# Two-layer transformer on one core: the sparse attention step reorganised around stacked query rows

## What is computed

```
proj = x @ w_q                                   # 1024 -> 1024 query columns + 48 gate columns
q = rmsnorm_2(proj[..., :1024].reshape(..., G, HG, dh), q_norm)        # 4 groups x 4 heads of 64
gates = sigmoid(proj[..., 1024:])                                      # per head and branch
s_c = q @ k_c.T * scale + head_bias(rel_c);  p_c = softmax(mask(s_c));  o_c = p_c @ v_c
s_s = q @ k_sel.T * scale + bias_s;          p_s = softmax(mask(s_s));  o_s = p_s @ v_sel
s_w = q @ k_wb.T * scale + head_bias(rel_w); p_w = softmax(mask(s_w));  o_w = p_w @ v_wb
out = (gates[0] * o_c + gates[1] * o_s + gates[2] * o_w) @ w_o;   h = h + out
```

## Time and profile before

| | us |
|---|---|
| median of 3 runs | 2265.68 |
| lowest and highest | 2264.12, 2272.57 |
| the profiled execution, own time | 2275.57 |
| its span, first to last instruction | 2274.3 |
| PE busy | 2192.8 (96%) |
| DVE busy | 1207.8 (53%) |
| ACT busy | 1012.2 (45%) |
| POOL busy | 15.5 (1%) |
| mean granted clock of TensorE | 0.96 of 2.4 GHz |

### The profile page before, as it was taken

The page is one execution under the profiler, slowest core; times in us unless marked ns, Lnnn a source line. Parts: engine busy times, 40 slices in busy tenths (PEclk is TensorE's granted clock), DMA queues, the critical chain, the costliest instruction groups (busy, mean ns, idle before and its releaser), DMA issues.

```text
span 2274.3 us, 25942 instructions
## 1 busy us (share of the span) xinstructions
PE 2192.8 (96%) x10555; PEld 1801.3 (79%) x10555; DVE 1207.8 (53%) x1350; ACT 1012.2 (45%) x1320; POOL 15.5 (1%) x33
## 2 busy tenths in 40 slices
PE   8998999999999999999999999999999998999999
PEld 6887987888888766888888798788768876768887
DVE  5455686545554645644654565545545554345544
ACT  6444345445444555534544433444444443435443
POOL 1000000000000000000000000000000000000000
PEclk9999999999999999999999999999999996558999
DMA  7553436564664522655565446756366541104653
GB/s 257 181 192 109 144 112 204 174 202 165 204 204 146 164 79 93 195 200 179 169 205 182 167 148 186 228 171 200 97 137 215 193 143 38 37 1 130 204 184 111
DMA packets 265378, 361.02 MB, mean 159 GB/s; under 512 B 19855, under 2 KB 206651, under 8 KB 265132
## 3 DMA queue, kind: packets, MB, share of 16 engines
q1 hardware_dynamic: 256800, 351.57, 47.1%
q10 hardware_dynamic: 7772, 7.17, 1.9%
q0 software_dynamic: 688, 0.62, 0.1%
HBM read 357.75 MB, written 1.57 MB: 158 GB/s over the span
## 4 chain that ended last, share of the span: by engine, by line
PE 89%; DVE 5%; ACT 3%; DMA 1%; issue 1%; ACTq 1%; SPq 0%; DVEq 0%
PE bank L384 18%; PE bank L386 17%; PE bank L385 17%; PE acc L646 6%; PE acc L645 6%; PE acc L644 6%; PE bank L379 2%; PE bank L380 2%; PE bank L381 2%; PE tr L625 2%; PE acc L1791 1%; PE bank L1757 1%; DMA raw_in<-ffn_w_in 1%; PE acc L675 1%; PE acc L677 1%; PE acc L676 1%
## 5 line engine op out<-in xcount | busy, mean ns | idle before, releaser
L384 PE MATMUL bank<-w_hi_,xt_hi_ 128*128 128x512 f32 x1792 | 725.2, 405 | 12.6 <-DVE h_tok L751 5.2
L386 PE MATMUL bank<-w_hi_,xt_lo_ 128*128 128x512 f32 x1792 | 704.4, 393 | 0.0
L385 PE MATMUL bank<-w_lo_,xt_hi_ 128*128 128x512 f32 x1792 | 703.6, 393 | 0.0
L408 DVE TENSOR_TENSOR w_lo_<-raw_in,w_hi_ 128x2048 fp32r<-128x2048 f32 (+1 forms) x315 | 571.0, 1820 | 241.1 <-ACT w_hi_ L398 240.8
L398 ACT ACTIVATE w_hi_<-raw_in 128x2048 fp32r<-128x2048 f32 (+1 forms) x315 | 478.5, 1533 | 91.8 <-PE bank L386 28.1
L756 DVE TENSOR_TENSOR wo_lo_<-raw_out,wo_hi_ 128x2048 fp32r<-128x2048 f32 x80 | 183.4, 2292 | 471.4 <-ACT wo_hi_ L721 471.4
L384 PEld LDWEIGHTS bank<-w_hi_,xt_hi_ 128*128 128x128 f32 x1792 | 340.1, 190 | 84.3 <-issue 6.4
L386 PEld LDWEIGHTS bank<-w_hi_,xt_lo_ 128*128 128x128 f32 x1792 | 339.6, 189 | 73.4
L385 PEld LDWEIGHTS bank<-w_lo_,xt_hi_ 128*128 128x128 f32 x1792 | 340.6, 190 | 63.2
L721 ACT ACTIVATE wo_hi_<-raw_out 128x2048 fp32r<-128x2048 f32 x80 | 153.3, 1916 | 358.8 <-PE acc L646 358.5
L644 PE MATMUL acc<-wo_hi_,ht_hi_ 128*128 128x512 f32 x576 | 224.1, 389 | 0.0
(11 more groups left out here) (271 smaller groups left out, 1850.5 us busy)
## 6 DMA issues: line engine op xcount, KB each, us to landing
raw_in<-ffn_w_in SPq DMA_DIRECT2D x352, 512.0 KB, 4.9
raw_out<-ffn_w_out SPq DMA_DIRECT2D x88, 1024.0 KB, 4.9
raw_in<-hg_w_in SPq DMA_DIRECT2D x16, 1024.0 KB, 5.3
raw_in<-fox_w_in SPq DMA_DIRECT2D x16, 1024.0 KB, 5.5
raw_in<-conv_w_in SPq DMA_DIRECT2D x12, 1024.0 KB, 5.2
raw_in<-hg_w_out SPq DMA_DIRECT2D x4, 1024.0 KB, 5.0
raw_in<-fox_w_out SPq DMA_DIRECT2D x4, 1024.0 KB, 5.1
raw_in<-conv_w_out SPq DMA_DIRECT2D x4, 1024.0 KB, 5.2
```

The costliest lines, as they stand in the source:

```text
L384: mm(o, g.xt_hi_[:, k, tok], wh[:, par, k, 0:w], start=first, stop=False)
L385: mm(o, g.xt_hi_[:, k, tok], wl[:, par, k, 0:w], start=False, stop=False)
L386: last = mm(o, g.xt_lo_[:, k, tok], wh[:, par, k, 0:w], start=False, stop=end)
L408: dve.e.tensor_tensor(g.piece(g.wl, n, half, k), raw, g.piece(g.wh, n, half, k).bitcast(F32), ALU.subtract).then_inc(g.w_lo, 4 if k is Non ...
```

## The change

The stage is written anew; the stages around it keep their code but for small items.

- **Stacked queries.** For a pair of heads PE transposes both tiles (`stack`), ACT writes the high part of a head's query to its 64 rows, DVE writes the low part to the other 64 rows of the same tile (`ns_queries`, in `hth` and `htl`). The keys of both branches, which lie twice one above the other, are split once: high into `oh` by four ACT copies, low into `ol` by four DVE subtractions. The scores of a head and tile are then two F32R products: 128 rows (both parts of the query with the high keys), both branches side by side, and 64 rows (the high query with the low keys). The compressed keys are split likewise (`kct2`), and their scores become four products of 16 columns per head in the unused part of the bank of tile 0.
- **One head per step.** A step ("time", 21 of them) has two halves: `values` of the head four times back and `turn` of the head three times back, then `scores` of the head before and `stack`. Each works on both tiles. One time stays empty for each kind after head 7.
- **Products between the heads.** The second query chunk stands beside times 0 to 6. At times 14 to 19 each half is followed by three matmuls of the output product, whose first half of terms (k = 0 to 3) needs only heads 0 to 7, transposed at time 12 (`turn_o`). After the last time come 12 more of these, the transposes of heads 8 to 15 and 48 matmuls. Times 7 to 13 have no product.
- **The rest.** DVE scales per head, with both tiles and branches in one instruction, and POOL adds the two branches (`pool_nsa`). The compressed branch is softmaxed, transposed and multiplied once for each half of the heads with both tiles together, and added by DVE. The splits of the output weights move to times 9 to 12; those of the first chunk of the next stage follow the output. The probabilities lie in `raw_out`, so SP waits before it loads the output weights of the last SwiGLU stage.

The core of the diff, in the order of the file: tiles and views, SP's wait, the compressed keys' low part on DVE, the step plan, then `pe_nsa`, `act_nsa`, `dve_nsa` and `pool_nsa`.

```diff
-        self.ns_qt = self.area(8768, KT, T)
...
-        self.ns_sbuf = self.area(12864, 2, 2, T)
...
+        self.ns_pt_ = [self.area(12864, 2, P), self.area(13120, 2, T)]
...
+        flat = self.raw_out[:].rearrange("p a b -> p (a b)")
+        self.ns_p = [[flat[:, i * 6 * P + t * 2 * P:][:, 0:2 * (t + 1) * P].rearrange("p (b n) -> p b n", b=2)
+                      for t in range(NT)] for i in range(2)]
...
+                if f == 7 and c == 1:
+                    sp.wait_ge(g.ns_turned, 2 * NSA_HEADS)
...
+    elif j == 16:
+        dve.wait_ge(g.kv_kct, 2)
+        dve.e.scalar_tensor_tensor(
+            g.kct2[:, :, 1, 0:n], g.tr[0][:, 0:GROUPS * NB_CMP].rearrange("p (g n) -> p g n", g=GROUPS)[:, :, 0:n],
+            g.gains[:, G_KN:G_KN + 1], g.kct2[:, :, 0, 0:n].bitcast(F32), ALU.mult, ALU.subtract).then_inc(g.kv_kct, 1)
...
+NS_TIMES = NSA_HEADS + 5
+NS_FIRST_OUT = 14
...
+def ns_head(time, lag):
+    at = time - lag
+    h = at if at < 8 else at - 1
+    return h if 0 <= h < NSA_HEADS and at != 8 else None
+
+
+def ns_part(time, part, stack, scores, turn, values):
+
+    for do, lag in ((values, 4), (turn, 3)) if part == 0 else ((scores, 1), (stack, 0)):
+        h = ns_head(time, lag)
+        if h is not None:
+            do(h)
...
+def ns_slot(part):
+
+    return lambda j: part((j - 2) // 2, j % 2) if j >= 2 else None
...
+def ns_queries(g, h):
+    return (g.hth, g.htl)[h // 2 % 2][:].rearrange("p (i a) n -> p i (a n)", i=2)[:, h % 2]
...
+def pe_out_k(g, pe, n, t, k, out, u):
+
+    pe.wait_ge(g.w_lo, 8 * n + 4 * (k // 4) + 4)
+    pe.wait_ge(g.xt_lo, 4 * u + 2 * (k // 4) + t + 1)
+    tok, mm = slice(t * P, (t + 1) * P), pe.e.matmul
+    mm(out[:], g.xt_hi_[:, k, tok], g.wh[:, n % 2, k, :], start=k == 0, stop=False)
+    mm(out[:], g.xt_hi_[:, k, tok], g.wl[:, n % 2, k, :], start=False, stop=False)
+    return mm(out[:], g.xt_lo_[:, k, tok], g.wh[:, n % 2, k, :], start=False, stop=k == KT - 1)
...
+    def stack(h):
+        if h % 2:
+            return
+        pe.wait_ge(g.hr_normed, J_NSA + 2 * (h // 8) + 2)
+        pe.wait_ge(g.ns_ql, h)
+        for t in range(NT):
+            ins = pe.e.transpose(g.tr[1][:, t * P:(t + 1) * P], tmp[:, t, h * DH:(h + 2) * DH], g.ident[:])
+        ins.then_inc(g.ns_stack, 1)
...
+    def scores(h):
+        gr, high = h * GROUPS // H, slice(DH * (h % 2), DH * (h % 2) + DH)
+        pe.wait_ge(g.ns_ql, h + 1)
+        pe.wait_ge(g.ns_csc, h)
+        if h == 0:
+            pe.wait_ge(g.ns_gt, 1)
+            pe.wait_ge(g.kv_kct, 3)
+        pe.wait_ge(g.ns_klo, gr + 1)
+        for t in range(NT):
+            q, n = ns_queries(g, h)[:, t * P:(t + 1) * P], (t + 1) * P
+            pe.wait_ge(g.ns_s, 2 * (h - 1) + t + 1)
+            o = score[t][:, 0:2 * n].rearrange("p (b n) -> p b n", b=2)
+            pe.e.matmul(o, q, ns_keys(g.oh)[:, :, gr, 0:n], start=True, stop=False)
+            ins = pe.e.matmul(o, q[high], ns_keys(g.ol)[high, :, gr, 0:n], start=False, stop=True)
+            if t == 0:
+                for tile in range(NT):
+                    q = ns_queries(g, h)[:, tile * P:(tile + 1) * P]
+                    o = score[0][:, T + tile * NB_CMP:T + (tile + 1) * NB_CMP]
+                    pe.e.matmul(o, q, g.kct2[:, gr, 0], start=True, stop=False)
+                    ins = pe.e.matmul(o, q[high], g.kct2[high, gr, 1], start=False, stop=True)
+            ins.then_inc(g.ns_sc, 1)
...
+    def turn(h):
+        for t in range(NT):
+            pe.wait_ge(g.ns_exp, 2 * h + t + 1)
+            pe.wait_ge(g.ns_pt, 2 * (h - 1) + t + 1)
+            if h == 0:
+                pe.wait_ge(g.ns_gates, 1)
+            if h >= 8:
+                pe.wait_ge(g.ns_cpt, 1)
+            n = (t + 1) * P
+            for br in range(2):
+                for b in range(t + 1):
+                    ins = pe.e.transpose(turned[t][:, br * n + b * P:br * n + (b + 1) * P],
+                                         g.ns_p[h % 2][t][:, br, b * P:(b + 1) * P], g.ident[:])
+            ins.then_inc(g.ns_turned, 1)
...
+    def values(h):
+        gr = h * GROUPS // H
+        pe.wait_ge(g.ns_pt, 2 * h + 2)
+        pe.wait_ge(g.ns_ob, h)
+        pe.wait_ge(g.kv_vv, 4)
+        for t in range(NT):
+            for br in range(2):
+                for b in range(t + 1):
+                    c = (2 * t + br) * DH
+                    ins = pe.e.matmul(pv[:, c:c + DH], g.ns_pt_[t][:, br, b * P:(b + 1) * P],
+                                      g.vv[:, br, b, gr * DH:(gr + 1) * DH], start=(b == 0), stop=(b == t))
+        ins.then_inc(g.ns_pv, 1)
...
+    out = [(c, t) for c in range(2) for t in range(NT)]
+    out_bank = [g.bank[0], g.bank[1], g.accs[0], g.accs[1]]
...
+    def part(time, half):
+        if (time, half) == (0, 0):
+            gates()
+        if (time, half) == (11, 0):
+            c_values(0, g.bank)
+        if (time, half) == (20, 0):
+            c_values(1, (g.tr[1], g.accs[1]))
+        ns_part(time, half, stack, scores, turn, values)
+        if (time, half) == (10, 1):
+            c_turn(0)
+        if (time, half) == (12, 1):
+            turn_o(0, g.bank)
+        if (time, half) == (19, 1):
+            c_turn(1)
...
-        pe_product(g, pe, n0 + 1, t, g.bank[0], u, slot=entry)
...
+    for time in range(7, NS_TIMES):
+        for half in range(2):
+            part(time, half)
+            i = 2 * (time - NS_FIRST_OUT) + half
+            if 0 <= i < 12:
+                out_k(i // 4, i % 4)
+    for k in range(4):
+        out_k(3, k)
+    turn_o(1, (g.tr[1], g.tr[0]))
+    for i in range(4):
+        for k in range(4, KT):
+            out_k(i, k)
...
+    for gr in range(GROUPS):
+        act.wait_ge(g.hr_done, J_KV + 4)
+        act.e.activation(ns_keys(g.oh)[:, :, gr], g.kt[:, :, gr], ACT.Copy).then_inc(g.ns_khi, 1)
...
+    def stack(h):
+        if h % 2:
+            return
+        act.wait_ge(g.ns_stack, h // 2 + 1)
+        act.wait_ge(g.ns_sc, 2 * (h - 2))
+        for odd in range(2):
+            high = slice(DH * odd, DH * odd + DH)
+            act.e.activation(ns_queries(g, h + odd)[high], g.tr[1][high, 0:T], ACT.Copy,
+                             scale=g.gains[high, G_NSAQ:G_NSAQ + 1]).then_inc(g.ns_qh, 1)
...
+    def turn(h):
+        for t in range(NT):
+            act.wait_ge(g.ns_turned, 2 * h + t + 1)
+            act.wait_ge(g.ns_pv, h)
+            act.e.activation(g.ns_pt_[t].rearrange("p b n -> p (b n)"), (g.tr[0], g.accs[2])[t][:, 0:2 * (t + 1) * P],
+                             ACT.Copy).then_inc(g.ns_pt, 1)
...
+    def stack(h):
+        if h % 2:
+            return
+        for odd in range(2):
+            q, high, low = ns_queries(g, h + odd), slice(DH * odd, DH * odd + DH), slice(DH - DH * odd, P - DH * odd)
+            dve.wait_ge(g.ns_qh, h + odd + 1)
+            dve.e.scalar_tensor_tensor(q[low], g.tr[1][high, 0:T], g.gains[high, G_NSAQ:G_NSAQ + 1],
+                                       q[high].bitcast(F32), ALU.mult, ALU.subtract).then_inc(g.ns_ql, 1)
...
+    def scores(h):
+        for t in range(NT):
+            n, s = (t + 1) * P, g.ns_p[h % 2][t]
+            dve.wait_ge(g.ns_sc, 2 * h + t + 1)
+            dve.wait_ge(g.ns_turned, 2 * (h - 2) + t + 1)
+            dve.wait_ge(g.tb_in, 16 * (P // COPIES))
+            dve.e.tensor_tensor(s, g.accs[t][:, 0:2 * n].rearrange("p (b n) -> p b n", b=2),
+                                g.tb[:, h, T - n:T].unsqueeze(1).to_broadcast([P, 2, n]), ALU.add).then_inc(g.ns_s, 1)
+            dve.wait_ge(g.ns_s, 2 * h + t + 1)
+            dve.e.tensor_reduce(g.ns_nm[:, t, :, h], s, AX.X, ALU.max, negate=True).then_inc(g.ns_m, 1)
+        dve.wait_ge(g.kv_cb, NT)
+        if h >= 8:
+            dve.wait_ge(g.ns_cturned, 1)
+        dve.e.tensor_tensor(g.ns_c[:, :, h % 8, :], g.accs[0][:, T:T + NT * NB_CMP].rearrange("p (t n) -> p t n", t=NT),
+                            g.cb[:, :, h], ALU.add).then_inc(g.ns_csc, 1)
...
+    def values(h):
+        den, coef = g.ns_den[:, :, :, h], g.coef[:, :, :, h]
+        dve.wait_ge(g.ns_exp, 2 * h + 2)
+        dve.wait_ge(g.ns_gates, 1)
+        dve.wait_ge(g.own_dve, dve.step(dve.e.reciprocal(den, den)))
+        dve.wait_ge(g.own_dve, dve.step(dve.e.tensor_tensor(coef, den, gates[:, :, h, 1:3], ALU.mult)))
+        dve.wait_ge(g.ns_pv, h + 1)
+        dve.wait_ge(g.ns_o, h - 1)
+        dve.e.tensor_tensor(g.ob[:, h % 2], g.accs[3][:, 0:T].rearrange("p (t b d) -> p t b d", t=NT, b=2),
+                            coef.unsqueeze(3).to_broadcast([P, NT, 2, DH]), ALU.mult).then_inc(g.ns_ob, 1)
...
+    for time in range(7, NS_TIMES):
+        for half in range(2):
+            part(time, half)
+            i = 2 * (time - 9) + half
+            if 0 <= i < 8:
+                dve_split(g, dve, n0 + 3, i // 4, i % 4)
...
+    def add(i, bank):
+        c, t = i // 2, i % 2
+        cols = slice(c * CW, (c + 1) * CW)
+        dve.wait_ge(g.prod, 2 * (n0 + 2) + i + 1)
```

(60 more changed lines are left out.)

397 lines of the change are left out of this document (122 added, 275 removed).

## The result

The changed kernel took 2237.1 us, median of 4 runs (2228.9 to 2240.8), against 2264.9 of 4 runs of the kernel before (2261.7 to 2272.6): a ratio of 0.9867, with a 95% interval of 0.983 to 0.9905. It is 27.8 us faster. 2217 was forecast, so it is 20 us slower than that, and inside the range of 2185 to 2257. It lies between the forecast's own band and the half-clock rival's 2242.

What follows compares the result with a forecast made beforehand. PE at half clock was taken to bound the sparse attention. The terms 3 + 3 + 42 + 45 + 42 + 15 = 150 us against 199, 49 less, gave 2265.7 - 49 = 2217 us, range 2185 to 2257.

Steps and rivals of the forecast that it cites:

- the forecast's own band: Time of the whole kernel: 2200 to 2235 us, chance 0.46.
- half-clock rival: Sparse attention at half clock until the last product: 175 us, 24 less, time 2242, chance 0.27.
- The stretch and its clock: Query product to next stage: 199 to 150 us, clock near 1.00 in first and third part, 0.50 between.
- full clock throughout: Sparse attention at full clock all through: 110 us, 89 less, time 2177, chance 0.12.
- the slower rival: Sparse attention bound by the loop through three queues: 9.5 us a time, 22 us more, 2287, chance 0.07.
- its point: The loop through three queues decides from 9.0 us a time on, 210 us in all.
- The scores: PE's score products per head: 2.1 us instead of 3.6 at half clock, 1.1 at full clock.
- Times 0 to 6: First stretch, with 48 product matmuls: 49 us at half clock, 25 at full, 42 taken.
- times 14 to 20: Third stretch, with the 12 matmuls after it: 60 us at half clock, 30 at full, 42 taken.
- The middle: Times 7 to 13, without products: 45 us at half clock.
- it stands 9.9 us above the median, which I carry over: Base of the time: profiled execution 2275.6 to 2227 us, its 9.9 us excess carried over, giving 2217.
- never the last releaser: POOL's sums of the two branches: under 1 us each, and never the last thing waited for.

Runs made afterwards that it cites:

- the repeat: Changed kernel run once more unaltered: 2238.2 us, ratio 0.9862; where 12.7 us is named, the kernel before run once more unchanged: 2272.9 us.
- the repeat of the kernel before: The kernel before run once more, unchanged, for a second trace: 2272.9 us.
- the sums swapped: Changed kernel with all score products on 128 rows, plus DVE's last residual sum moved ahead of its last weight split: 2220.1 us, ratio 0.9792.

## Why the prediction was right in the stretch and 20 us off in the time

**The stretch and its clock: right.** 199.2 became 150.9, 150 was forecast. The clock is full in both stretches with products, but for 10 us of the first, and half between them in this trace (for 37.5 of 47.8 us in the repeat), as written. Moving the output products away shows that they hold the level in the third stretch. The half-clock rival fell at 1995; full clock throughout fell in the middle. The loop of the slower rival, 9.5 us a time, stayed below its point: the dearest seven times took 53.6 us, 7.7 each, and they hold the compressed branch too.

**The scores: mis-sized.** The forecast took 1.1 and 2.1 us a head from rows in which 128-row weights follow each other; measured are 2.1 and 3.4. The bounds it gave for this, -12 to +3 us, were for the small products alone and didn't see the rows. At 128 rows the scores cost 1.16 and 2.2, the forecast's own price, and that version is 13 to 16 us shorter in the stretch. The rows to see it were in the trace of before, where fox changes between 64 and 128 rows; the forecast took only others from there.

**The choice within each stretch: too low on the clock.** Times 0 to 6 (42 chosen between 49 and 25) came out at 37.3 at a mean clock of 0.87, times 14 to 20 (42 between 60 and 30) at 39.3 at 0.91, though the scores in them were dearer than the forecast had them. That gave back 7.4 us, and the scores and round trips of the middle took 8.6. The middle was priced with PE at half clock and no waits (45). It took 53.6 with PE idle for 5.2 us. The errors of the sum cancelled, so its hitting 150 is luck and not a proof of its terms.

**What the sum left out: the border behind it.** The forecast asked what comes late in the stretch, and not what comes late at its end. The last SwiGLU stage takes 194.2 us where it took 191.1: 3.1 us given back.

**The base: the failed step of the time.** "it stands 9.9 us above the median, which I carry over" treats the excess as one that is the same in both kernels. It isn't: the profile of after stands 3.6 us above its median. And the stretch to be replaced is where executions differ most: the repeat of the kernel before, 2.7 us shorter in all, has 12.7 us less in it. What the stretch takes in an execution at the median no trace shows. From profile to profile the fall is 34.8 us, not 49:

- the stretch lost 48.1 (from the narrow product to the next stage, 198.8 to 150.7)
- the stage before it had the other clock pattern: +7.0 (204.4 to 211.4)
- it began 3.4 later (1663.0 to 1666.4; it did so at 1666.0 in the repeat of the kernel before, so this is not the change's either)
- the last SwiGLU stage: +3.1.

48.1 - 13.5 = 34.6. With the 6.3 us between 9.9 and 3.6, 13.5 + 6.3 = 19.8, which is the miss. Of these, 3.1 is the change's; the pattern of the stage before it comes in both kernels (below). Against the repeat of the kernel before, whose stage before nsa ran with the pattern of the changed kernel, the stretch lost 35.4 and 38.7 us and the spans 32.3 and 35.1; the medians say 27.8. Had all 9.9 us been taken from the stretch, where the repeat finds 12.7, the same sum would have said 2265.7 - 39.3 = 2226.

**POOL: right but for the last head.** 0.45 us lies within the forecast 0.3 to 1.0. Fifteen sums were hidden. The last one was to be "never the last releaser" like the others, and it stands in the chain that ended last, with DVE's last sums behind it, before PE goes on:

```profile
2025.70 0.46 POOL arena L2059
...
2026.18 1.30 DVE arena L2011 x2
```

The version with all score products on 128 rows is the best of those run: 2220.8 and, with the sums swapped, 2220.1 us, 2% below the kernel before. Beside the same kernel before, the version with the sums swapped stands at 0.9792 [0.9768, 0.9816] and the change at 0.9862 [0.9834, 0.9891]; the intervals do not meet.

What stays open: why the clock of the stage before nsa takes one of two patterns. The kernel before took 204.4 and 211.5 us there, the change 211.4 and 211.5, versions of it that differ only behind that stage 204.1, 204.2, 204.6, 211.4 and 211.5. The runs don't tell what decides, but it is decided early: the six traces with the long form, of both kernels, also show 3.4 us at 0.50 near 1387 us, and none of the four with the short form does. Nor is it settled why the medians fell by 28 us where the traces nearest to each other say 32 to 35; one execution of each is too little for that. The recorded clocks point at the choice of execution: 13 spans of the kernel before go from 2255.5 us at a mean granted clock of 0.972 to 2275.2 at 0.959, in that order throughout, and its two traces have 0.960 and 0.962, so both are of the slower ones.

## What to carry to other kernels

Before a change is priced from one profile, ask in which stage that execution was slow: where a clock moves, two profiles of one kernel tell what is the kernel's, and here 12.7 us of the stretch were the execution's. Between matmuls count the changes of the number of weight rows and not only the columns; redundant rows were cheaper here than fewer rows. Products put between short attention products held the clock here, and that pays only as long as PE is what bounds; then ask what the product that became shorter used to cover behind it.

## What the runs showed of the hardware that was not expected

- A load of 64 weight rows next to one of 128 does not run under the product before it: products of 512 columns stand 0.42 us apart at 1.00, and 0.24 to 0.34 when all have 128 rows; of 16 columns 0.20 and 0.11. At 0.50 those of 512 columns are 0.72 to 0.74 and 0.44 to 0.63 apart. Between two loads of 64 rows the overlap stays (fox stage of the kernel before, 834.16 to 834.48).
- POOL's sum took 0.45 or 0.46 us in 14 of 16 heads and 0.84 and 0.83 in two, at 1960.22 and 1971.65. Both times DVE was in a split that reads two tiles of SBUF (0.68 us, its usual length). In the version with 128 rows it is again two of 16 (0.83), again beside such a split. The Trainium skill's rule of the shared port pair ("SBUF — State Buffer", section "SBUF: two separate sides") says that the one that comes second blocks, and the trace agrees with it: POOL was that one. The price is 0.4 us each, off the path, where the forecast allowed for up to 8 us in all.
- The same kernel spends 6.8 or 23.9 us of one SwiGLU stage at half clock, 7 us of difference. In the 23.9 us of the changed kernel PE was busy for 21.99.
